# Moving the four router-weight loads on ScalarE's queue from ahead of the last-branch merge to behind it

## The reference

```
hm = mlstm(...);  hd = diff_attention(...)
merged = sigmoid(g_m) * (hm @ w_br_m) + sigmoid(g_d) * (hd @ w_br_d)
x  = x + gate1 * (merged @ w_out)
h2 = rmsnorm(x, norm2_w) * (1 + scale2) + shift2

# hierarchical mixture of experts on h2: 4 groups of 8 experts, 2 experts of one group for each token
g_logits = h2 @ w_rg + b_rg            # w_rg is 1024 x 4
e_logits = h2 @ w_re + b_re            # w_re is 1024 x 32
...choose the group, then its two best experts, and their weights...
y = sum over experts e of combine[:, e] * ((silu(h2 @ w_gate[e]) * (h2 @ w_up[e])) @ w_down[e])
x = x + gate2 * y
```

## Time and profile before

| | us |
|---|---|
| median of 3 runs | 1348.92 |
| the three runs | 1348.2, 1348.92, 1353.29 |
| the profiled execution, its own time | 1353.29 |
| its span in the trace | 1351.5 |
| PE busy | 1237.1 (92% of the span) |
| DVE busy | 567.2 (42%) |
| ACT busy | 310.4 (23%) |
| POOL busy | 247.3 (18%) |
| DMA moved | 213.01 MB, mean 158 GB/s |

### The profile page before, as it was taken

The page is one execution under the profiler, slowest core; times in us unless marked ns, Lnnn a source line. Parts: engine busy times, 40 slices in busy tenths (PEclk is TensorE's granted clock), DMA queues, the critical chain, the costliest instruction groups (busy, mean ns, idle before and its releaser), DMA issues.

```text
span 1351.5 us, 13279 instructions
## 1 busy us (share of the span) xinstructions
PE 1237.1 (92%) x4904; PEld 686.9 (51%) x4904; DVE 567.2 (42%) x1468; ACT 310.4 (23%) x725; POOL 247.3 (18%) x214
## 2 busy tenths in 40 slices
PE   7899989999989999999999986999999879977875
PEld 3455434445544444688864443777764534432322
DVE  3114483467558731239943358322232623221221
ACT  3213643433210001231132343200011311110110
POOL 7000022354500000163300000422300022111100
PEclk9999999999989999999999897999999979988888
DMA  9525122323365530404230220012247579999993
GB/s 322 106 71 125 63 72 53 109 69 134 115 201 183 187 123 34 156 1 153 96 125 1 63 62 1 5 63 63 63 171 327 218 287 404 402 409 405 410 359 92
DMA packets 92678, 213.01 MB, mean 158 GB/s; under 512 B 20233, under 2 KB 51225, under 8 KB 80791
## 3 DMA queue, kind: packets, MB, share of 16 engines
q1 hardware_dynamic: 79088, 190.98, 38.6%
q0 software_dynamic: 10176, 17.96, 5.4%
q10 hardware_dynamic: 3344, 3.16, 0.7%
HBM read 205.69 MB, written 14.75 MB: 163 GB/s over the span
## 4 chain that ended last, share of the span: by engine, by line
PE 71%; SPq 9%; DVE 9%; DMA 5%; ACT 2%; issue 2%; POOL 0%; ACTq 0%; POOLq 0%; DVEq 0%
SPq L2705 9%; PE PS L2238 7%; PE PS L964 6%; PE PS L1379 4%; PE PS L1457 4%; PE PS L2820 4%; PE PS L1640 4%; PE PS L1642 4%; PE PS L2297 4%; PE PS L2388 3%; PE PS L609 3%; PE PS L1686 2%; PE PS L1388 2%; PE PS L1995 2%; DMA X<-in_w_up 2%
## 5 line engine op out<-in xcount | busy, mean ns | idle before, releaser
L964 PE MATMUL PS<-HT,W 128*128 128x512 f32 x256 | 126.0, 616 | 1.8 <-ACT AN L1128 1.7
L1226 POOL TENSOR_SCALAR AN<-AN,SM 128x128 f32<-128x128 f32 (+3 forms) x64 | 72.2, 1137 | 202.7 <-DVE SM L1318 202.7
L2820 PE MATMUL PS<-AN,HT 128*64 128x512 f32 x272 | 87.9, 652 | 17.5 <-DMA X<-in_w_up 8.4
L1249 DVE SCALAR_TENSOR_TENSOR AN<-AN,COLA 128x256 f32<-128x256 f32 x168 | 85.1, 507 | 5.0
L609 PE MATMUL PS<-W,HT 128*128 128x512 f32 (+1 forms) x192 | 72.2, 538 | 0.0
L2899 DVE TENSOR_TENSOR HT<-HT,PS 128x256 f32<-128x256 f32 x16 | 6.7, 421 | 152.8 <-ACT HT L2877 152.8
L2820 PEld LDWEIGHTS PS<-AN,HT 128*64 128x64 f32 x272 | 28.8, 150 | 72.9 <-issue 72.9
L964 PEld LDWEIGHTS PS<-HT,W 128*128 128x128 f32 x256 | 45.0, 195 | 39.7 <-issue 36.1
L1379 PE MATMUL PS<-HT,W 128*128 128x512 f32 x128 | 58.1, 599 | 0.0
L2219 POOL TENSOR_TENSOR AN<-W 128x512 f32<-128x512 f32 x8 | 10.5, 1311 | 258.6 <-PE PS L2078 186.6
L2388 PE MATMUL PS<-W,AN 128*128 128x512 f32 x128 | 57.6, 597 | 0.0
(11 more groups left out here) (508 smaller groups left out, 2239.9 us busy)
## 6 DMA issues: line engine op xcount, KB each, us to landing
W<-in_w_in SPq DMA_DIRECT2D x14, 2048.0 KB, 8.8
W<-in_w_down SPq DMA_DIRECT2D x20, 1024.0 KB, 23.6
AN<-in_w_ada SPq DMA_DIRECT2D x17, 1024.0 KB, 5.3
AN<-in_w_gate SPq DMA_DIRECT2D x15, 1024.0 KB, 19.0
AN<-in_w_up SPq DMA_DIRECT2D x15, 1024.0 KB, 29.1
AN<-in_w_down SPq DMA_DIRECT2D x12, 1024.0 KB, 19.4
W<-in_w_gate SPq DMA_DIRECT2D x10, 1024.0 KB, 22.7
W<-in_w_up SPq DMA_DIRECT2D x10, 1024.0 KB, 29.3
```

Of the source, the lines that this page charges most:

```text
L964: t = pe.matmul(u.ap, w[:, c, tile(m)], hT[:, c, :], start=c == 0, stop=c == 7)
L1226: pool.tensor_scalar(PU[u % 5][:, 0:n], PU[u % 5][:, 0:n], RSUM[:, u:u + 1], None, ALU.mult).then_inc(*sc_pool.up(u))
L1249: dve.scalar_tensor_tensor(out=a, in0=wt[:, c, :], scalar=ca["c2"][:, c:c + 1], in1=a, op0=ALU.mult, op1=ALU.add).then_inc(*ada_dve.up(p, c))
L2820: t = pe.matmul(u.ap[r, :].rearrange("p (n f) -> p n f", n=2), XGT[e % 2][:, c, r], w_gu(3 * e + half)[:, c], start=c == 0, stop=c == 7)
```

## The change

`act_wr` is no longer called in `act_merge2` but in `scalar_program`, between `act_merge2` and `act_out2`, and its two waits (for the product mv (3, 3) of the mLSTM stage, and for `hd_act.at(3, 3)`) give place to one, for p2 (7, 1). The four loads and the readers' waits are as they were.

```diff
@@ act_merge2
     def act_merge2(act, wa):
         wa.wait_ge(*hd_act.at(3, 3))
         act.activation(HR3[:, 16:32], HS3[:, 16:32], ACT.Sqrt, bias=eps, scale=1.0 / 128).then_inc(*om_act.up("root2"))
-        act_wr(act, wa)
         wa.wait_ge(*set_dve.at("sub"))
@@ act_wr
     def act_wr(act, wa):
-        wa.wait_ge(*B.use("mv", 3, 3).full)
-        wa.wait_ge(*hd_act.at(3, 3))
+        wa.wait_ge(*B.use("p2", 7, 1).full)
         act.dma_start(WR[:, :, 0:4], A["w_rg_2"][0].rearrange("(c p) n -> p c n", p=128)).then_inc(*wr_in.up())
         act.dma_start(WR[:, :, 4:36], A["w_re_2"][0].rearrange("(c p) n -> p c n", p=128)).then_inc(*wr_in.up())
@@ scalar_program
         act_merge2(act, wa)
+        act_wr(act, wa)
         act_out2(act, wa)
```

## The result

| | before | after |
|---|---|---|
| median of the timed runs, us | 1350.23 (1348.20 to 1353.29, 4 runs) | 1383.65 (1380.99 to 1384.66, 4 runs) |
| profiled execution: own time / span, us | 1353.29 / 1351.5 | 1387.88 / 1386.1 |
| granted clock, mean over the span | 0.958 | 0.946 |
| first product group with w_out starts, us | 1004.12 | 1005.37 |
| first pair of experts starts, us | 1091.07 | 1124.10 |

The changed kernel takes 1.0243 times as long, 95% interval 1.0216 to 1.0269: 33.4 us, where 27.8 were forecast; as a time, 1383.65 us, where 1377 was. Its profiled execution was 3 to 7 us above the timed ones.

What follows compares the result with a forecast made beforehand. PE was taken to bound out2 without a break, so a stall there moves everything after. Removal 0, stall 25.5 and clock 2.3 sum to 27.8 us over a median of 1348.92: 1377 us forecast, range 1365 to 1384.

Steps and rivals of the forecast that it cites:

- The removal is worth 0: Old place near 851 us: the loads hold nobody up there, so taking them away gains 0; other bound 2.2 us.
- The time of issue: New place: ACT, idle there, issues at 1004.2; the four issues take 2.2 us and don't make its own work late.
- Turns of one to one: Queues of ACT and SP from 1005.2: they alternate by packet of any size; the loads need 148 turns an engine.
- The first rival: Queues at the new place: several small packets go to a turn; no loss, 1349 to 1350 us; chance 10%.
- The end of the stall: PE at the router's bias: waits from 1010.4 to 1035.9, a stall of 25.5 us; bounds 0 and 26.5.
- The clock: PE's restart after the stall: half speed at first, costing 2.3 us, bounds 0 to 4.6; back some 4 us after restart.
- Nothing given back: Experts' stage: 0 of the stall is recovered; as a rival, half comes back, 1363 us, chance 4%.
- The sum: Whole kernel: 0 + 25.5 + 2.3 = 27.8 us slower, against the median of 1348.92 giving 1376.7, predicted as 1377 us.
- the 1371 to 1382 that the terms gave: Whole kernel: the forecast's own range, from stall 24 to 26.5, clock 0 to 4.6, and about 2 us run spread.

Runs made afterwards that it cites:

- packed: The changed kernel, but the four arrays are copied early into one DRAM area and loaded late in rows of 1296 bytes; 1353.27 us, 1.0009 of before.
- before_gate7: Against the kernel before, the loads moved to ahead of ACT's last gate pair, with their old waits; 1351.81 us, 1.0000 of before.
- seam_p6: The changed kernel, but the loads wait for p2 (6, 1), one product group earlier, instead of p2 (7, 1); 1378.16 us, 1.0187 of before.
- seam_no_wait: The changed kernel, but the loads keep their old two waits instead of the one for p2 (7, 1); 1359.59 us, 1.0051 of before.
- experts_after: The changed kernel, but SP issues no expert load until the router's loads have landed; 1358.66 us, 1.0036 of before.
- after_again: The changed kernel measured once more, without any edit; 1386.42 us, 1.0260 of before.
- twice: The changed kernel, but w_rg and w_re are first also loaded into another area at the same place; 1386.74 us, 1.0260 of before.

## Why the prediction was right, and where a size was off

**The removal is worth 0: right.** packed keeps an early copy at the old place and before_gate7 has nothing there; both equal before, the first with 0.9987 to 1.0032, the second with 0.9983 to 1.0018.

**The time of issue: right.** 1005.41 with the seam at 1005.37, as forecast (ACT is idle there). That the issues themselves would take 2.2 us was wrong: 16.3 (1005.41 to 1021.69), for the queue was full. Nobody waited for ACT, so it cost nothing.

**Turns of one to one: right in place, not everywhere.** In the windows shown of after and of seam_p6 the counts are equal to a packet. The Trainium skill, in "DMA: Bandwidth & Descriptors", section "Queues, rings and completion order", has an engine drain some 9 to 17 descriptors before it switches. Equal counts over 4 us would not exclude equal bundles, but short windows do. These are the queues of after from 1012.25 to 1012.5, about one packet an engine:

```profile
q1 hardware_dynamic: 16, 0.10, 97.4%
q10 hardware_dynamic: 17, 0.00, 4.5%
```

In all sixteen windows of 0.25 us from 1012 to 1016 the two counts differ by 2 at most, and in the ten of 0.1 us from 1020 to 1021 by 1. Counted in the profile's packets (2368, for 2304 rows and 16 more for each load), the two queues went one by one here, not in bundles of nine. The page has it otherwise, and the measurement decides. The first rival, several tiny ones to a turn, is excluded for a full q1. packed shows from the other side what 9 packets an engine pay: 5.5 us. That the full q1 is a condition I had not seen; seam_no_wait taught it.

**The end of the stall: right in mechanism, 1.8 us short.** I had ACT's first packet at 1.0 us after the issue; it came after 3.6. Up to 1008.8 alone q1 had 592 packets, 37 an engine, without a turn for the other. At 1034.3 the router's loads still had 629 packets to go (148 + 481), 39 an engine. The two stalls measured, 27.34 and 26.71, passed the upper bound of 26.5 by 0.8 and 0.2, but stayed near it for the reason given: q1 runs dry at 1037 and the rest goes alone. 25.5 was taken.

**The clock: the term that was mis-sized.** Taken 2.3, bounds 0 to 4.6; measured 4.44 and 3.24. I took the loss of the first expert group from the earlier trace rows, whose slow stretch had begun before that group, and so counted only a part of the way back. Here the clock was at 0.50 from the first product on: the bias took 3.60 us instead of 1.71, the next group 9.34 instead of 6.95, and this makes 4.28. I had also said that it would be back 4 us after the restart; it was 8.3, and 6.0 to 7.7 in the seven other traces with a stop of 2.56 us or more. The loss at the restart does not grow with the stop: 3.4, 3.6, 3.6 and 4.0 us after stops of 2.56, 4.54, 4.87 and 11.35, then 3.2, 3.2, 4.3 and 3.3 after 25.89, 26.71, 27.34 and 29.05. After 0.57 and 1.04 it was 0.2 and 0.3.

**Nothing given back: right.** From the first pair of experts to the end of the span it is 260.4 us before and 262.0 after, and between 259.5 and 262.1 in all others. experts_after excludes the stage's transfers as a bound of the seam's size: they started 7 us later against the seam, and the end did not.

**The sum.** 27.8 forecast, and 1377 as a time. The measured 1383.65 lies beyond the 1371 to 1382 that the terms gave, and only 0.35 us inside the range stated, 1365 to 1384: the mechanism was right, but that the time still fell inside is partly luck. In the profiled executions, whose spans differ by 34.6: 27.34 + 4.44 = 31.8 at the seam, and 2.8 (1.25 ahead, 1.6 behind) that no step had. By the medians it is 33.4, by after_again 35, of which its trace has 30 at the seam. Part of the gap between 27.8 and 33 is thus the clock (2.1) and the wait (1.8); the 1.25 ahead of the seam come from the first 850 us, which the change does not touch (the square root starts at 852.17 against 850.91), and the rest I can't assign.

## What to carry to other kernels

Before a load is moved, count its packets an engine, and look whether a full queue runs beside the new place: in these runs the price was packets times the other queue's time for one (0.27 us beside the experts' loads), up to that queue's backlog, and the bytes of the moved load did not enter. Four remedies were measured: few long rows (no loss), a place before the burst (no loss), the queue of the burst itself, ahead of it (7 us instead of 33), or the burst held back until the loads have landed (5 us). And each stop of PE, of 2.6 us or more in these runs, cost 3.2 to 4.3 us more than itself in clock.

## What the runs showed of the hardware that I had not expected

- Equal turns hold only beside a queue that is always ready: 1064 small packets to 270 at the start of a burst, 563 to 563 in its middle. In the middle of after's they are turns of a single packet: in each quarter of a microsecond from 1012 to 1016 the two queues start 10 to 27 packets over 16 engines, equal to within 2.
- An issue can block its engine while its queue moves slowly: 12.57 us for the third issue, behind some 130 packets an engine, and 14.0 us twice in twice. The length alone is not the reason: before, the same third issue began when 25 of those packets had started, and took 0.63 us. It ended with 884 started there, and with 890 in after. Here ACT had time; on an engine with work it would be a stall of its own.
- The first packet beside SP's busy queue came 3.4 to 3.8 us after the issue in nine traces, alone 1.0 to 1.2. That delay does not follow the other queue's turns: SP's queue started 315 packets in it in seam_p6 and 712 in twice. What it is stays open.
- The loss at the clock behind a restart does not grow with the stop: 3.4 us after a stop of 2.56 us, 4.3 and 3.2 after 27.34 and 26.71 in two traces of one kernel, and 0.3 after 1.04.
